# Scattering the dense tiles' gates into DRAM and making 96 chunks of their activations while experts are chosen

## What is computed

```
v1, i1 = lax.top_k(s1, 16); v2, i2 = lax.top_k(s2, 16)          # keys of each half, 8 heads
cand = (v1[..., :, None] + v2[..., None, :]).reshape(n, 8, 256)
sc, sel = lax.top_k(cand, 16)
idx = take_along_axis(i1 * 128 + i2, sel);  gate = softmax(sc)
h = einsum('nhkd,nd->nhk', peer_u[idx], x)
a = gelu(h) * gate
out = einsum('nhk,nhkd->nd', a, peer_v[idx])
```

## Time and profile before

| what | us |
|---|---|
| median of three runs (2322.49 to 2333.73) | 2329.89 |
| the profiled execution | 2326.4 |
| its span | 2324.6 |
| VectorE busy | 1387.1 |
| TensorE busy | 1911.5 |
| the dense pass, 1190 to 2325 | 1135 |

### The profile page before, as it was taken

One profiled execution on the slowest core, in us unless ns is written; L12 is line 12 of the kernel. 1 busy time (PEld: TensorE's weight loads), 2 busy tenths in 40 slices (PEclk: granted clock), 3 DMA queues, 4 the chain that ended last, 5 costly groups with the idle time before them and its releaser, 6 DMA issues.

```text
span 2324.6 us, 23161 instructions
## 1 busy us (share of the span) xinstructions
PE 1911.5 (82%) x7719; PEld 1267.5 (55%) x7719; DVE 1387.1 (60%) x3062; ACT 602.6 (26%) x1194; POOL 807.5 (35%) x858
## 2 busy tenths in 40 slices
PE   6979976688997923557779889889899999999996
PEld 4667653354553502334446556566566666666763
DVE  7540368775336398886528697556456555555553
ACT  1123010242121103568932122112122122111221
POOL 0172003444333333233200036445445455454520
PEclk9979978798998956578799899999999999999998
DMA  5332346667675644466544578999889999999972
GB/s 207 86 93 78 127 145 235 219 229 241 213 302 195 221 145 134 173 228 252 199 161 130 163 277 340 350 336 407 328 311 390 343 407 382 359 388 384 353 286 72
DMA packets 167509, 574.80 MB, mean 247 GB/s; under 512 B 17248, under 2 KB 36112, under 8 KB 165952
## 3 DMA queue, kind: packets, MB, share of 16 engines
q0 software_dynamic: 93328, 340.78, 40.2%
q1 hardware_dynamic: 71136, 210.53, 25.3%
q10 hardware_dynamic: 2928, 22.02, 2.5%
HBM read 552.27 MB, written 20.46 MB: 246 GB/s over the span
## 4 chain that ended last, share of the span: by engine, by line
PE 64%; DVE 14%; ACT 8%; DMA 8%; issue 5%; POOL 0%; ACTq 0%; SPq 0%; DVEq 0%
PE bank L922 17%; PE bank L912 16%; PE bank L799 8%; DMA wring<-in_pv 6%; PE bank L866 4%; PE bank L904 4%; PE bank L820 3%; ACT region L1409 3%; ACT discretisation L1631 3%; PE bank L839 2%; PE bank L712 2%; PE bank L895 1%; PE bank L620 1%; DVE region L1323 1%; DMA wring<-in_w 1%
## 5 line engine op out<-in xcount | busy, mean ns | idle before, releaser
L570 POOL DMA_INDIRECT region<-in_pu,region x320 | 421.7, 1318 | 1083.2 <-DVE region L1323 824.4
L922 PE MATMUL bank<-wring,hgT 128*128 128x512 f32 x1024 | 479.0, 612 | 36.3 <-DMA wring<-in_pv 36.2
L912 PE MATMUL bank<-xT,region 128*128 128x256 f32 x2048 | 471.2, 384 | 0.0
L912 PEld LDWEIGHTS bank<-xT,region 128*128 128x128 f32 x2048 | 385.4, 193 | 49.0 <-issue 0.5
L1409 ACT ACTIVATE region<-bank 128x512 f32<-128x512 f32 (+4 forms) x383 | 249.7, 652 | 578.2 <-PE bank L904 444.1
L1323 DVE CUSTOM_DVE_ANT_0 region<-region 128x1024 f32<-128x1024 f32 x320 | 388.6, 1221 | 13.3 <-DMA region<-in_pu,region 11.8
L922 PEld LDWEIGHTS bank<-wring,hgT 128*128 128x128 f32 x1024 | 191.4, 197 | 233.4 <-issue 195.2
L1363 DVE TENSOR_TENSOR hgT<-hgT,region 128x256 f32<-128x256 f32 x128 | 54.4, 425 | 422.4 <-ACT hgT L1658 367.2
L577 POOL DMA_INDIRECT region<-in_pv,region x256 | 254.3, 993 | 134.5 <-issue 75.8
L1313 DVE SCALAR_TENSOR_TENSOR region<-region 128x1024 f32<-128x1024 f32 x189 | 243.9, 1291 | 4.1 <-issue 3.0
L866 PE MATMUL bank<-region,small 128*128 128x512 f32 x256 | 160.5, 767 | 93.7 <-ACT small L1604 69.0
(11 more groups left out here) (256 smaller groups left out, 1942.1 us busy)
## 6 DMA issues: line engine op xcount, KB each, us to landing
wring<-in_pu SPq DMA_DIRECT2D x128, 512.0 KB
wring<-in_pv SPq DMA_DIRECT2D x128, 512.0 KB
wring<-in_w SPq DMA_DIRECT2D x104, 512.0 KB, 4.7
gates_by_chunk<-region ACTq DMA_DIRECT2D x8, 2048.0 KB
region<-gates_by_chunk SPq DMA_DIRECT2D x16, 1024.0 KB
region<-in_pu,region POOLq DMA_INDIRECT x320
region<-in_pv,region POOLq DMA_INDIRECT x256
out_y<-region ACTq DMA_DIRECT2D x4, 512.0 KB, 2.6
```

Source lines behind the costliest of these rows:

```text
L570: pool.indirect_dma_start(ring_u[q % U_RING], None, io["pu"], bass.IndirectOffsetOnAxis(ind[:, k:k + 1], 0)).then_inc(g_u[q % U_RING], 16)
L912: last = mm(b[:, 0:DT], UT[c % 2][:, k, :], xT[:, k, D0:TOK], start=k == 0, stop=k == KT - 1)
L922: last = mm(b[:, :], A[c % 2][:, 128 * j:128 * j + 128], w[:, 512 * hf:512 * hf + 512], start=c == 0, stop=c == CHUNKS - 1)
```

## The change

- The gates of the dense tiles are no longer made by one-hot rows. A matrix of 16,384 experts by 256 tokens in DRAM (16.8 MB) is filled with zeros at the start, by eight DMAs from ScalarE's queue. `choose` works out the flat address expert x 256 + token for each gate, and GpSimd adds each column of 128 gates to the matrix with an indirect DMA that accumulates (`scatter`): 2 tiles x 128 columns = 256 DMAs of 128 elements of 4 bytes. The first of each head waits for all of the heads before it to have landed. The items `gt` and `g` are gone.
- `tr` and `h` of chunks 0 to 95 run while experts are chosen. The gelu's result, 128 x 256, is stored to DRAM by ScalarE (`early_activations`, 12.6 MB) and comes back in the dense pass, where item `m` on VectorE multiplies it with the gates. There only `v` is left of these chunks. Chunks 96 to 127 run as before. Transposes alternate between two banks and there are three buffers for the transposed rows, three for gelus and four for the activations.
- The choice moves: tile 0 into the mix, tile 3 half into the mix's end, then the rest of tile 3, tile 4 and tile 2 in the new choice stage. None is left for the dense pass.
- The slots are placed by stage: 92 in the mix, 108 in the choice, the rest in the dense pass. The lag between a slot's dot and its v row grows (`ADD_LAG` 8 to 13), the rings are 6 and 7 rows after slot 91, and VectorE adds three of four v rows of tile 1 instead of half.
- `top` works on both key halves in turn, so that one's wait lies under the other's work.

```diff
-SELECT = [1, 3, 4, 0, 2]
+SELECT = [1, 0, 3, 4, 2]
-ACT_LAG, GATE_LAG, DIAG_LAG, ADD_LAG = 5, 6, 7, 8
-V_LAG = 4
+ACT_LAG, GATE_LAG, DIAG_LAG, ADD_LAG = 5, 9, 10, 13
+V_LAG = 9
-HOTS, BLOCK, GROUP = 4, 32, 8
-U_RING, V_RING = 4, 5
+GROUP = 4
+U_PLACES, V_PLACES = (4, 6), (5, 7)
+AHEAD_CHUNKS = 96
+SLOTS_MIX, SLOTS_SELECT = 92, 108
...
-    return q >= 96 + 32 or (q < 96 and q % 2 == 1)
+    return q >= 128 or q % 4 != 0
...
+            def scatter(t, h, i):
+                j = DENSE.index(t)
+                pool.wait_ge(idx_s, 2 * SELECT.index(t) + 1 + h // 4)
+                if h and i == 0:
+                    pool.wait_ge(g_out[j], 16 * TOPK * h)
+                for k in range(TOPK * h + 4 * i, TOPK * h + 4 * i + 4):
+                    pool.indirect_dma_start(all_gates, bass.IndirectOffsetOnAxis(goes[j][:, k:k + 1], 0), gd[j][:, k:k + 1], None,
+                                            compute_op=ALU.add).then_inc(g_out[j], 16)
...
             def do_ut():
+                act.wait_ge(zeros_s, 1)
+                for i in range(8):
+                    act.dma_start(all_gates.rearrange("(i p n t) one -> i p n (t one)", i=8, p=128, t=DT)[i],
+                                  zeros.unsqueeze(1).broadcast_to([128, 16, DT])).then_inc(zeroed, 16)
...
-                drain(("h", c), S.activation(hg[c % 2], b[:, 0:DT], ACT.Gelu))
+                drain(("h", c), S.activation(hg[c % 3], b[:, 0:DT], ACT.Gelu))
+                if c < AHEAD_CHUNKS:
+                    act.dma_start(acts_out[c], hg[c % 3]).then_inc(h_out[c % 3], 16)
...
+            def do_m(c):
+                g = c // GROUP
+                dve.wait_ge(h_in[g % 2], 16 * (g // 2 + 1))
+                activations(c, acts[g % 2][:, c % GROUP, :])
```

More of the change, by code:

```diff
@@ L124, in schedule @@
[L124 to L128, removed]
-            q += 1
[L130 to L135, removed]
@@ L136, in schedule @@
-    for c in range(CHUNKS):
[L137 to L142, removed]
+    fold = selection(0)
+    fold[0].insert(0, ("sc", 0, 0))
+    fold[9].append(("fold",))
+    for entry in mix:
+        if entry[0][0] == "gates" or (entry[0][0] == "merge" and entry[0][2] >= 2):
+            entry += fold.pop(0) if fold else []
@@ new lines, in schedule, with spread @@
+    assert not fold
+    mix = [(first.pop(0) if first else []) + entry for entry in mix]
+    wq = len(mix) - 4
+    mix[wq] += [("sc", 3, 0), ("top", 3, 0)]
+    for n in range(1, 4):
+        mix[wq + n].append(("top", 3, n))
+    q = 0
+    def spread(entries, until):
+        nonlocal q
+        out, first, at, total = [], q, 0, sum(SPAN[item[0]] for entry in entries for item in entry)
+        for entry in entries:
+            while q < until and (q - first) * total <= at * (until - first):
+                out += slot_items(q)
+                q += 1
+            out += entry
+            at += sum(SPAN[item[0]] for item in entry)
+        while q < until:
+            out += slot_items(q)
+            q += 1
+        return out
@@ new lines, in schedule @@
+    s += spread(mix, SLOTS_MIX)
+    chunks = [[("tr", 0, 0), ("tr", 0, 1), ("tr", 1, 0), ("tr", 1, 1)]]
+    for c in range(AHEAD_CHUNKS):
+        chunks.append([("tr", c + 2, 0), ("h", c), ("tr", c + 2, 1)] if c + 2 < AHEAD_CHUNKS else [("h", c)])
+    select = []
+    for t, nxt in ((3, 4), (4, 2), (2, None)):
+        part = selection(t)
+        if t == 3:
+            part = part[4:]
+        if nxt is not None:
+            part[-1].insert(0, ("sc", nxt, 0))
+        select += part
+    parts = [("scatter", t, h, i) for t in DENSE for h in range(NH) for i in range(4)]
@@ new lines, in schedule @@
+    for n in range(2, 26):
+        for k in range(3):
+            if parts and (n >= 1 + 5 * (parts[0][2] // 4) + 10 * DENSE.index(parts[0][1]) + 1):
+                select[n].append(parts.pop(0))
+    assert not parts
+    for n, entry in enumerate(select):
+        take = -(-len(chunks) // (len(select) - n))
+        entry += [x for chunk in chunks[:take] for x in chunk]
+        chunks = chunks[take:]
+    s += spread(select, SLOTS_MIX + SLOTS_SELECT)
+    first, end, at = q, NQ + ADD_LAG, 0
@@ L143, in schedule @@
+    spans = [2.9 if c < AHEAD_CHUNKS else 10 for c in range(CHUNKS)]
+    total = sum(spans) - 25
+    s += [("m", 0), ("m", 1)]
+    for c in range(CHUNKS):
+        s += [("m", c + 2)] if c + 2 < AHEAD_CHUNKS else []
+        s += [("tr", c + 3, 0)] if AHEAD_CHUNKS <= c + 3 < CHUNKS else []
+        s += [("h", c + 2)] if AHEAD_CHUNKS <= c + 2 < CHUNKS else []
+        while q < end and (q - first) * total <= at * (end - first):
+            s += slot_items(q)
             q += 1
-            if q == 192 + ADD_LAG:
-                s += [("fold_sum",), ("final", 0)]
@@ L1597, in slot_work @@
                 j = q - DIAG_LAG
[L1598 removed]
+                if 0 <= j < NQ and not on_dve[j]:
                     d = by_pe[j] - 1
```

354 lines of the change are left out of this document (165 added, 189 removed).

## The result

The changed kernel takes 2372.54 us (median of four runs, 2368.31 to 2377.49), beside 2329.51 of the kernel before (four runs). The ratio is 1.0189, 95% interval 1.0152 to 1.0225. The forecast was 2185 with a range of 2050 to 2320: wrong in sign, and outside the range.

The account below looks back on a forecast made before the run. GpSimd was to bound the choice stage and the DMA the dense pass: 849 to the mix's end, 656 choice, 10 first gates, 650 dense pass, 18 end, plus 1.8 to execution, gave 2185 us, range 2050 to 2320.

Parts of the forecast that it names:

- the price of a scatter: Choice stage, GpSimd: each of 256 scatters costs 1.25 us like an unbroken gather, 320 us in all.
- The rival's turning point: Choice stage: scatter price from which the rival of dearer scatters (1.8 us or more, kernel slower than before) decides, 1.80 us.
- the chance of 0.12: Whole kernel: chance given to a time over 2338 us, slower than before.
- the rival's 2.05: Choice stage: at 2.05 us a scatter the stage is 861 us and the kernel 2390; slower had chance 0.12.
- The waits for landing: Choice stage, GpSimd: a head's first scatter waits for the last to land, nine places, 4.3 plus 0.8 us each, 46.
- the uneven entries: Choice stage: in four entries without scatters VectorE is slower than GpSimd by about 5 us each, 20 in all.
- the first gates: Ahead of the dense pass: the first gates and gelus wait for all scatters, 10 us.
- Ahead of the mix: Start of the kernel, 357 us before: writing the zeros makes streamed weights late by 3 us, between 0 and 45.
- The mix: Stage before the choice, 445 us before: three parts of 196, 155 and 138 us, ending at 849.
- The clock: Choice stage, TensorE: clock falls to about 0.73, costing nothing while 445 us over the clock stays under 656.
- The dense pass: Last main stage: the DMA is the bound, 240.7 MB at 372 GB/s, 650 us; TensorE needs 579, VectorE about 350.
- Nearly free scatters: Choice stage rival: DMA at 473 or VectorE at 440 bounds it, 520 with uneven entries, kernel 2050; chance 0.18.

Follow-up runs that it names:

- e2_plain_write: Changed kernel with the 256 scatters writing plainly instead of accumulating: 2331.8 us, beside 2368.5 for the changed kernel's profiled execution.
- e9_half_addresses: Changed kernel with 64 addresses in each accumulating scatter instead of 128, half of the gates left out: 2346.1 us.
- e3_big_zeros: Changed kernel with the same 16.8 MB of zeros written from a wide zeroed tile, 16 KB in a row instead of 1 KB pieces: 2329.1 us.
- e8_zeros_and_128: Changed kernel with zeros in 16 KB rows and 128 chunks made ahead instead of 96: 2296.75 us, ratio 0.9882 to the kernel before.
- e1_no_scatter: Changed kernel with all 256 scatters left out, so the matrix of gates stays zero: 2021.6 us.

## Why the prediction was wrong

**The step that failed** is the price of a scatter, taken as that of an unbroken gather, 1.25 us. Without its waits for landing, 27.4 us (22.9 and one more of 4.4 that the trace puts down to "issue"), it is (531 - 27.4)/256 = 1.97: 256 x 0.72 = 184 us more. The argument was that a scatter has 128 addresses to be turned into transfers, as a gather has. e2_plain_write shows that this is true of a plain scatter (0.97 against 0.94), and that accumulating adds 0.58; the mean of 1.67 lies over the median because 18 in 100 take 1.9 us or more. The rival's turning point was 1.80, and the chance of 0.12 on that side was too small. No row showed an accumulating DMA; the price taken, 1.25, and the upper end, 2.05, lay on both sides of that point, and nothing but likeness spoke for the lower one.

That the rival's 2.05 came so near to 1.97 is luck. It was the price of a gather after a wait, 1.75, and that slower start hardly occurs: of the nine scatters that waited, eight take 1.55 to 1.64. Of its two reasons, more work for each address is 0.13 us for 64 addresses (e9_half_addresses), and no run shows the queue filling up. Two more terms of that stage:

- The waits for landing: 46 in the forecast, 27.4 in nine places measured. They are 2.1 to 4.9 us instead of 4.3, and the slower start of 0.8 behind them came once.
- 217 gathers: forecast 290 with the uneven entries, measured 316 (the four other rows of the groups). Of their idle time 21 us are waits for dots and sums.

So 184 - 19 + 26 = 191 on GpSimd over the whole of 847, against 181 in the table for choice and first gates: some of the last gathers lie in what the forecast called the first gates.

**Ahead of the mix** the forecast had 3 for the zeros and it was 33. It asked what 16.8 MB cost the DMA engines, and for the queue that issues them it put nothing. e3_big_zeros shows that the engines' time is indeed hidden and the queue's isn't.

**The mix** took 459 and not 489. This error of -30 hides the +30 ahead of it, so that the first `h` came at the very 849 that was forecast: a mark that is right for two wrong reasons. The parts of the forecast, parted at the third `merge` (573) and behind the last (703), take 183, 130 and 146 us where it had 196, 155 and 138. In the middle part the forecast summed 151 us of VectorE's work and took that as the bound; 119 stand there, so work passed over the border into the last part:

```profile
573.00:703.00 130.00, 108.85 (x338) 61.15 (x336) 119.43 (x324) 29.94 (x42) 63.07 (x54) 0.92 0.78 292
```

**The clock** fell to 0.78, about as said, and cost nothing, as said: TensorE's 495 us of busy time lie far under 847.

**The dense pass** was right in its bound and its length: 650 us, 371 GB/s over all of it (372 taken), with TensorE at 601 where 579 was summed and VectorE at 363 (350). The 36 us for which TensorE waited for `peer_v` are still there. The 358 GB/s of the Trainium skill, "DMA: Bandwidth & Descriptors", section "Specifications", would have given 672 by an estimate, and the trace disagrees once more: 371 GB/s here, and 398 over 500 us of e8_zeros_and_128. A note in the section "Bandwidth" of the same page ties this figure to two cores that stream at once; here one core runs. The waits of the changed kernel's dense pass, and the window of e8_zeros_and_128:

```profile
PE bank L969 <- DMA wring<-in_pv: 36.1, 11, 8.2
```

```profile
1700.00:2200.00 500.00, 385.19 (x810) 164.99 (x811) 310.18 (x473) 6.19 (x31) 281.12 (x225) 0.88 1.03 398
```

**Nearly free scatters** fell with the result, but e1_no_scatter shows that the bound of that rival, 520 for the stage, was sound (493 measured; kernel 2050 forecast, 2021.6 measured).

**Where the gain went.** It is there in e1_no_scatter: the 388 + 1135 us of before are 493 + 680 with its end (1340 to 2020), 350 less. The scatters take 354 back, in a stage in which every other resource has room, the dense pass gives 9, and the mix ends 47 later. That is 42, by which the profiled executions differ.

## What to carry to other kernels

Where a change brings hundreds of instructions of a kind that no row shows, their price is the prediction: work out the price at which the sign turns, and if it lies between the two bounds, let the chances say so. A transfer had two prices here, the bytes on the DMA engines and the time on the queue that issues it, and the second one stood in front of everything else on that engine: hand over long rows. When one engine is the bound of a stage, put other engines' work into it (128 chunks ahead instead of 96 cost 13 us and gave 50), and test a gain by a part at a time, since one edit of three may bring nothing.

## What the runs showed of the hardware

- An indirect DMA costs GpSimd 0.94 us as a gather of 128 rows, 0.97 as a plain scatter of 128 single numbers and 1.55 (mean 1.67) as an accumulating one, each with 0.30 until the next. With 64 addresses the accumulating one still costs 1.42. An accumulating one shows about one packet under 512 bytes for each address, a plain one about 18 for its 128.
- A DMA of 2,048 pieces of 1 KB occupies ScalarE's queue for about 5 us (40.45 for eight); of 128 rows of 16 KB about 1.1 us (7.60 for seven).
- Plain 4-byte scatters made other engines late without a recorded cause (328 and 292 us of ScalarE's waits, "remote", in two runs); accumulating ones didn't (10 us). Not explained.
- The DMA engines moved 371 to 380 GB/s over whole dense passes of 599 to 650 us, with one core running.
